# A PEER expert-choice stage: adaLN products spread between the key projections, and one-hot gate rows from a 16-bit comparison shared out anew

## The chip, the cores and the metric

The program runs on one core of one Trainium2 chip. Its engines work side by side and wait for each other by semaphores: TensorE (PE; its weight loads are PEld), VectorE (DVE), ScalarE (ACT), GpSimd (POOL), and SyncE (SP), which here only issues DMAs. The metric is the device time of one execution in microseconds (us). The numbers of before are the median of three timed executions, and one further execution taken by the profiler.

## The reference

One denoising step of a two-layer transformer over 640 tokens (512 latent, 128 context). Each layer has an attention mixer (differential attention in layer 0, latent attention in layer 1), then a PEER mixer: product-key retrieval of 16 experts out of 16384 for each of 8 heads. Each sub-layer is an RMS norm with a shift, a scale and a gate (adaLN) from a linear map of the conditioning vector. The part that matters here:

```python
def modulation(cvec, w, b):
    m = jax.nn.silu(cvec) @ w + b
    return [t[:, None, :] for t in jnp.split(m, 6, axis=-1)]

def peer(h, wq, sub_keys, u, v):
    ...
    def one(xb):
        q = (xb @ wq).reshape(TOK_BLOCK, PEER_HEADS, 2, PEER_HALF)
        s = jnp.einsum('thcd,hcnd->thcn', q, sub_keys, preferred_element_type=jnp.float32)
        top_s, top_i = lax.top_k(s, PEER_TOPK)
        ...
        fs, fi = lax.top_k(cand_s, PEER_TOPK)
        idx = jnp.take_along_axis(cand_i, fi, axis=-1)
        g = jax.nn.softmax(fs, axis=-1)
        ue = u[idx]
        a = jax.nn.gelu(jnp.einsum('td,thkd->thk', xb, ue, preferred_element_type=jnp.float32))
        ve = v[idx]
        return jnp.einsum('thk,thkd->td', (g * a).astype(xb.dtype), ve)
```

## The kernel before

Tokens lie in five blocks of 128 (`TB = 5`). Each layer runs a norm, its attention, a second norm, `expert_choice`, and `experts`. The last takes most of the time: for the first 384 tokens (`TD`) it computes all 16384 experts with matmuls and weights them by a gate table in DRAM, for the other 256 it gathers the chosen rows. `expert_choice` chooses the experts and builds that table. It has two stages, and every engine has its own hand-written instruction order in it.

**Selection.** TensorE runs 20 key projections, `project` (L1336), n = 0 to 19, four for each block of tokens. Each is 32 matmuls of 128x128 in f32. In the middle of projection n it also does `scores` (L1350) of projection n-1. ScalarE copies the queries (`query`, L1411) and the scores (`score`, L1419) out of PSUM; at n = 4, 9, 14 and 19 it also writes two look-up tables (`tables`, L1428), and at n = 8, 12, 16 and 20 an exponential (`exps`, L1439). VectorE runs `choose` for each block: top 16 of 128 scores in four chunks c (L1569 to L1585), then the candidates (L1595), the ranks (L1599), top 16 of the candidates, and `lookups` (L1549, L1550). GpSimd finishes the lookups of blocks 0 to 3 (L1500, L1503, L1505) from the tables; block 4's are done by VectorE. `finish` (L1529 to L1534) normalizes the gates of the block before, in the middle of `choose`.

**The adaLN halves.** Twelve pieces ("halves") of layer 1's adaLN map are computed in layer 0's `expert_choice` (`early`, h = 0 to 11), four in layer 1's. One half is `late_half`: 8 matmuls of 128x256 into 32 PSUM partitions each (`mod_rows`, L119), whose result ScalarE copies to `mrow` (`late_row`, L1435), and which two small matmuls then turn into columns (`late_turn`, `mod_turn`, L125). SyncE loads a half (1 MB, L1310) once the half two before it has been used. In the kernel before, all of them stand on TensorE behind the last projection and its scores; ScalarE copies four of them before the exponential of block 3, three before the tables of block 4, five after. VectorE adds the bias (L130) after its last block.

**Gate steps.** Then 32 steps (`STEPS`), each for 12 tokens (`SUB`), build the table. For every token a step needs two matrices of 128x128, which TensorE multiplies (L1388, 12 matmuls): `one1`, a comparison of first key numbers with 0 to 127 (tile `w`), and `one2`, the same for the second key numbers, times the gates (tile `pqT`). `one1` is VectorE's (L1651). Of the 12 tokens of `one2`, VectorE does 2 whole (L1649) and compares 6 more (L1645), which ScalarE scales by the gates (L1450), and GpSimd does 4 (L1512). ScalarE moves the product to a staging tile (`evict_g`, L1462), behind the scaling of the next step in its order; each pair of steps goes to DRAM as one DMA of 1.5 MB (L1318). There are two buffers of each operand and of the staging tile. With six steps to go (after pair 12 of 0 to 15) SyncE also starts two loads of 1 MB for the next stage (L1321).

The comparisons are in f32, and read the numbers 0 to 127 from PSUM (`iota_ps`) on VectorE and from SBUF (`iota`) on GpSimd.

Of the kernel before, what the change touches and what calls it, by code (L numbers as in the profile page):

```python
# [25 lines left out]
P = 128  # L26
# [34 lines left out]
def mixed(nc, cst, inp, outs, g_dram, x_dram):  # L61
# [1215 lines left out]
    def expert_choice(l, w3, pqT, keysT, selT, rows, gates, steps, sc, s2, cand, c2, vals, idxu, posu, idxp, ranks, posh,  # L1277
                      shift, fs, first, eq, tabs, sel, mrow):

# [14 lines left out]
        with nc.Block() as block:  # L1294
# [29 lines left out]
            def _(pe):  # L1324
# [40 lines left out]
                def late_turn(h):  # L1365

                    at = h - early[0]
                    pe.wait_ge(sem("late_row"), h + 1)
                    mod_turn(pe, ps[:, 7, 256 + 4 * at:260 + 4 * at], mrow[:, h % 2, :]).then_inc(sem("late_t"), 1)
# [37 lines left out]
            def _(act):  # L1407
# [22 lines left out]
                def late_row(h):  # L1430

                    act.wait_ge(sem("late_mm"), h + 1)
                    if h >= 2:
                        act.wait_ge(sem("late_t"), h - 1)
                    act.copy(mrow[:, h % 2, :], ps[:, 4 + 2 * (h % 2), 0:256]).then_inc(sem("late_row"), 1)  # L1435

# [40 lines left out]
                for h in early[4:7]:  # L1477
                    late_row(h)
                tables(TB - 1)
                for h in early[7:]:  # L1480
                    late_row(h)
                act.wait_ge(sem("late_t"), early[-1] + 1)
                act.copy(iota_ps, iota[:]).then_inc(sem("gm_iota"), 1)
# [11 lines left out]
            def _(pool):  # L1495
# [10 lines left out]
                for r in range(STEPS):  # L1506
                    t0 = r * SUB
                    pool.wait_ge(sem(n_ + "selT"), (t0 + SUB - 1) // P + 1)
                    if r >= 2:
                        pool.wait_ge(sem("gm_mm"), r - 1)  # L1510
                    for t in range(DIRECT + SCALED, SUB):
                        last = pool.tensor_scalar(one2[:, r % 2, t, :], iota[:], selT[:, 1, t0 + t:t0 + t + 1],  # L1512
                                                  selT[:, 2, t0 + t:t0 + t + 1], ALU.is_equal, ALU.mult)
                    last.then_inc(sem("gm_pool"), 1)

            @block.vector
            def _(v):
# [120 lines left out]
                def gate_step(r):  # L1638
                    t0 = r * SUB
                    v.wait_ge(sem("gm_iota"), 1)  # L1640
                    v.wait_ge(sem(n_ + "selT"), (t0 + SUB - 1) // P + 1)
                    if r >= 2:
                        v.wait_ge(sem("gm_mm"), r - 1)
                    n = SCALED
                    v.tensor_tensor(one2[:, r % 2, DIRECT:DIRECT + n],  # L1645
                                    selT[:, 1, t0 + DIRECT:t0 + DIRECT + n].unsqueeze(2).to_broadcast([P, n, P]),
                                    iota_ps.unsqueeze(1).to_broadcast([P, n, P]), ALU.is_equal).then_inc(sem("gm_eq"), 1)
                    for t in range(DIRECT):
                        v.tensor_scalar(one2[:, r % 2, t, :], iota_ps, selT[:, 1, t0 + t:t0 + t + 1],  # L1649
                                        selT[:, 2, t0 + t:t0 + t + 1], ALU.is_equal, ALU.mult)  # L1650
# [16 lines left out]
                v.wait_ge(sem("late_t"), early[-1] + 1)  # L1667
                add_bias(v, 1, k0, k0 + 2 * len(early), ps[:, 7, 256:256 + 4 * len(early)]).then_inc(sem("mod_v"), 1)
                if l == 0:
# [279 lines left out]
    def expert_layer(l):  # L1949
        with ExitStack() as st:  # L1950
# [3 lines left out]
            with ExitStack() as s2:  # L1954
# [7 lines left out]
                              sb(s2, f"first{l}", [P, 2, 16, 16], F16), sb(s2, f"eq{l}", [P, 2, HP, 16, 16], F16),  # L1962
                              sb(s2, f"tabs{l}", [P, 2, HP, 16, 16], F16), sb(s2, f"sel{l}", [P, TB, 2, HP, 16]), sb(s2, f"mrow{l}", [P, 2, 256]))

# [219 lines left out]
```

## Time and profile before

| what | us |
|---|---|
| median of three timed executions | 3924.34 |
| their range | 3922.66 to 3928.52 |
| the profiled execution | 3924.41 |
| its span, first to last instruction | 3922.6 |
| `expert_choice` of layer 0: projections start / first gate comparison / last gate matmul ends | 558.7 / 773.4 / 880.9 |

Rows come from the profiled execution, in us from the start of the span. The profile's page gives busy shares (PE 95%, DVE 83%, ACT 45%, POOL 28% of the span), which are means over stages with different limits. This stage is read in three kinds of view: windows, which give each engine's busy time and the granted clock of TensorE in a stretch; the timeline, which gives instructions in order with the idle time ahead of them and what ended it; and groups by line with the mean duration of one instruction. In the timeline a matmul in f32 shows as two records.

### The profile page before, as it was taken

What the parts mean: (1) busy time and instruction counts of PE and PEld (TensorE: products, weight loads), DVE (VectorE), ACT (ScalarE), POOL (GpSimd) and SP (SyncE); (2) the same over time, 40 slices, a digit from 0 to 9 for tenths busy, and PEclk for the clock granted to TensorE, in tenths of its full rate; (3) what the DMA queues carried; (4) which work ended last, traced back from release to release, by engine and by line L of the source; (5) the groups of instructions that cost most, each with busy time, mean ns of one, the idle gap of its engine ahead of it and who ended that gap; (6) DMA issues with size and microseconds to landing.
All of it is one profiled execution on the core that took longest, in us unless ns stands there. A gap on an engine that the chain in (4) does not pass through costs nothing. (4 is left out here: it accounts for less than half of the span.)

```text
span 3922.6 us, 55734 instructions
## 1 busy us (share of the span) xinstructions
PE 3731.2 (95%) x20637; PEld 3146.4 (80%) x20637; DVE 3239.0 (83%) x6793; ACT 1758.5 (45%) x2888; POOL 1117.1 (28%) x836
## 2 busy tenths in 40 slices
PE   8999999888999999999989999996899999999999
PEld 4546789688999999999854646896889999999998
DVE  5737639898999999999963636399899999999998
ACT  3315522394444444444423646223944444444443
POOL 0000003493333333333200000035833333333332
PEclk9999889799999999999989999897999999999999
DMA  7310030299999999999841010301999999999997
GB/s 300 140 43 12 22 128 2 108 251 409 421 413 408 405 406 404 404 405 406 326 175 52 1 43 22 128 2 51 266 426 418 413 409 404 404 406 403 406 405 296
DMA packets 268270, 1033.70 MB, mean 264 GB/s; under 512 B 147072, under 2 KB 150080, under 8 KB 159936
## 3 DMA queue, kind: packets, MB, share of 16 engines
q0 software_dynamic: 77184, 562.07, 35.7%
q1 hardware_dynamic: 190816, 468.07, 31.4%
q8 instruction: 165, 2.70, 0.3%
q14 instruction: 105, 0.86, 0.1%
HBM read 970.69 MB, written 59.39 MB: 263 GB/s over the span
## 5 line engine op out<-in xcount | busy, mean ns | idle before, releaser
L1727 POOL DMA_INDIRECT gbuf<-in_uv,rows x340 | 514.8, 1514 | 863.6 <-DVE hT L1911 793.8
L1911 DVE SCALAR_TENSOR_TENSOR hT<-gbuf,act,hT 128x1024 f32<-128x1024 f32 x336 | 416.9, 1282 | 6.0
L1896 DVE SCALAR_TENSOR_TENSOR gbuf<-gbuf,ht 128x1024 f32<-128x1024 f32 x340 | 402.0, 1219 | 11.5 <-DMA gbuf<-in_uv,rows 11.5
L1727 POOL DMA_INDIRECT xT<-in_uv,rows x172 | 256.9, 1494 | 473.0 <-DVE hT L1911 393.2
L1500 POOL TENSOR_TENSOR eq<-eq,tabs 128x4096 f16<-128x4096 f16 x8 | 63.5, 7940 | 1070.2 <-DVE eq L1550 981.3
L1743 PE MATMUL ps<-h0h,U0h 128*128 128x384 f32 x1024 | 345.0, 337 | 6.8 <-DVE U0l L1870 6.8
L1743 PE MATMUL ps<-h1h,U1h 128*128 128x384 f32 x1024 | 345.2, 337 | 6.0 <-DVE U1l L1870 6.0
L1743 PE MATMUL ps<-h1h,U1l 128*128 128x384 f32 x1024 | 344.5, 336 | 0.0
L1743 PE MATMUL ps<-h0h,U0l 128*128 128x384 f32 x1024 | 344.4, 336 | 0.0
L1743 PE MATMUL ps<-h1l,U1h 128*128 128x384 f32 x1024 | 344.3, 336 | 0.0
L1743 PE MATMUL ps<-h0l,U0h 128*128 128x384 f32 x1024 | 344.2, 336 | 0.0
L1816 ACT ACTIVATE ring<-ps 128x384 f32<-128x384 f32 x256 | 125.9, 492 | 392.4 <-PE ps L1743 392.3
L1826 ACT ACTIVATE act<-act 128x2 f32<-128x2 f32 x256 | 51.8, 202 | 444.7 <-DVE gbuf L1896 296.4
L1336 PE MATMUL ps<-hT,ring 128*128 128x128 f32 x1920 | 232.5, 281 | 6.1 <-ACT hT L317 4.5
L1336 PEld LDWEIGHTS ps<-hT,ring 128*128 128x128 f32 x1920 | 225.1, 196 | 10.8 <-ACT hT L317 5.7
L1388 PE MATMUL ps<-pqT,w 128*128 128x128 f32 x1536 | 190.6, 282 | 37.2 <-DVE w L1651 32.3
L1388 PEld LDWEIGHTS ps<-pqT,w 128*128 128x128 f32 x1536 | 180.5, 196 | 47.7 <-DVE w L1651 28.0
L1512 POOL TENSOR_SCALAR pqT<-iota,selT 128x128 f32<-128x128 f32 x256 | 203.8, 810 | 51.1 <-ACT selT L1443 28.4
L1896 DVE SCALAR_TENSOR_TENSOR xT<-xT,ht 128x1024 f32<-128x1024 f32 x172 | 203.5, 1220 | 9.6 <-DMA xT<-in_uv,rows 9.6
L1911 DVE SCALAR_TENSOR_TENSOR hT<-xT,act,hT 128x1024 f32<-128x1024 f32 x168 | 208.4, 1282 | 3.0
L1743 PEld LDWEIGHTS ps<-h0h,U0h 128*128 128x128 f32 x1024 | 193.5, 189 | 10.0 <-DVE U0l L1870 7.5
L1743 PEld LDWEIGHTS ps<-h1h,U1h 128*128 128x128 f32 x1024 | 193.9, 189 | 9.1 <-DVE U1l L1870 6.6
(392 smaller groups left out, 9150.3 us busy)
## 6 DMA issues: line engine op xcount, KB each, us to landing
ring<-in_u SPq DMA_DIRECT2D x128, 1024.0 KB, 12.5
ring<-in_v SPq DMA_DIRECT2D x128, 1024.0 KB
ring<-in_wts SPq DMA_DIRECT2D x26, 2048.0 KB, 8.8
gates<-ring SPq DMA_DIRECT2D x32, 1536.0 KB, 7.3
ring<-gates SPq DMA_DIRECT2D x64, 768.0 KB
abuf<-in_ada_mid POOLq DMA_DIRECT2D x16, 1024.0 KB, 5.1
xT<-in_ada_late SPq DMA_DIRECT2D x16, 1024.0 KB, 4.9
abuf_c<-in_ada_late POOLq DMA_DIRECT2D x8, 1024.0 KB, 5.1
```

The source lines that it names most:

```text
L1336: mm = pe.matmul(ps[:, 5 + n % 3, q * P:(q + 1) * P], w[:, dc, q * P:(q + 1) * P], hT[:, dc, tb * P:(tb + 1) * P], start=dc == 0, stop=dc ...
L1388: mm = pe.matmul(ps[:, b + t // 4, (t % 4) * P:(t % 4 + 1) * P], one1[:, r % 2, t, :], one2[:, r % 2, t, :], start=True, stop=True)
L1500: pool.tensor_tensor(eq4, eq4, tab4, ALU.mult).then_inc(look, 1)
L1512: last = pool.tensor_scalar(one2[:, r % 2, t, :], iota[:], selT[:, 1, t0 + t:t0 + t + 1], selT[:, 2, t0 + t:t0 + t + 1], ALU.is_equal, ALU ...
L1727: pool.indirect_dma_start(out=slots[m % GSLOTS], out_offset=None, in_=inp[f"uv{l}"], in_offset=bass.IndirectOffsetOnAxis(ap=rows[:, c:c + ...
L1743: mm = pe.matmul(up_bank(k), Us[x][:, k, dc * P:(dc + 1) * P], hs[y][:, dc, :], start=dc == 0 and x + y == 0, stop=dc == DC - 1 and x == 1)
L1816: act.activation(Wf[:, k, :], up_bank(k), ACT.Gelu_apprx_tanh).then_inc(sem(n_ + "gelu"), 1)
L1826: act.activation(act4[:, n % 2, 0:2], act4[:, n % 2, 0:2], ACT.Gelu_apprx_tanh)\
L1896: v.scalar_tensor_tensor(u, u, 1.0, ht[:, m // P, :], ALU.mult, ALU.mult, accum_out=act4[:, n % 2, m % 2:m % 2 + 1]).then_inc(sem(n_ + "do ...
L1911: v.scalar_tensor_tensor(y, x, w, y, ALU.mult, ALU.add).then_inc(sem(n_ + "acc"), 1)
```

## The change

Two edits in `expert_choice`.

The halves: `late_half(h)` now stands behind a projection, the first behind n = 6 (`FIRST_HALF`), one behind each after it: n = 6 to 17 in layer 0, n = 6 to 9 in layer 1. `late_half` begins with `late_turn` of the half before it. On ScalarE, `late_row` of a half stands behind `query` of the projection after it. All halves use PSUM bank 4.

The gate steps: VectorE compares 10 tokens at once in 16 bits (`hot`, in the space of `eq`), with the key numbers in `sel16` and the numbers 0 to 127 repeated ten times in `numbers`, both in SBUF. `hot` is laid out with the token innermost, so one token's 128 values lie 20 bytes apart. ScalarE scales tokens 0 to 3 from it, GpSimd tokens 4 to 9 in one multiplication with the gates broadcast, VectorE does tokens 10 and 11 whole as before. VectorE's new comparison waits for the readers of `hot` two steps back; its other work and ScalarE's scaling wait for the matmuls two steps back.

```diff
-        SUB, DIRECT, SCALED = 12, 2, 6
+        SUB, SCALED, HOT = 12, 4, 10
+        hot = eq[:].rearrange("p a h s k -> p (a h s k)")[:, 0:2 * P * HOT].rearrange("p (b n t) -> p b n t", b=2, n=P)
+        numbers = sc[:, 1].bitcast(F16).rearrange("p i k -> p (i k)")[:, 0:P * HOT].rearrange("p (n t) -> p n t", n=P)
+        FIRST_HALF = 6
...
                 def late_half(h):
 
-                    pe.wait_ge(sem(f"late_in{h % 2}"), 16 * (h // 2 + 1))
-                    if h - early[0] >= 2:
-                        pe.wait_ge(sem("late_row"), h - 1)
-                    mod_rows(pe, ps[:, 4 + 2 * (h % 2), 0:256], halves[:, h % 2]).then_inc(sem("late_mm"), 1)
                     if h != early[0]:
                         late_turn(h - 1)
+                    pe.wait_ge(sem(f"late_in{h % 2}"), 16 * (h // 2 + 1))
+                    mod_rows(pe, ps[:, 4, 0:256], halves[:, h % 2]).then_inc(sem("late_mm"), 1)
...
                     pe.wait_ge(sem("gm_one"), r + 1)
-                    pe.wait_ge(sem("gm_pool"), r + 1)
                     pe.wait_ge(sem("gm_scaled"), r + 1)
...
                     for t in range(SUB):
+                        if t == SCALED:
+                            pe.wait_ge(sem("gm_pool"), r + 1)
+                        if t == HOT:
+                            pe.wait_ge(sem("gm_direct"), r + 1)
...
                 for n in range(4 * TB):
                     project(n // 4, n % 4)
+                    if 0 <= n - FIRST_HALF < len(early):
+                        late_half(early[n - FIRST_HALF])
                 scores(TB - 1, 3)
-                for h in early:
-                    late_half(h)
...
                     act.wait_ge(sem(n_ + "t"), tb + 1)
+                    act.copy(sel16[:, tb * P:(tb + 1) * P], ps[:, 5, P:2 * P])
...
                     act.wait_ge(sem("gm_eq"), r + 1)
-                    for t in range(DIRECT, DIRECT + SCALED):
-                        at = act.activation(one2[:, r % 2, t, :], one2[:, r % 2, t, :], ACT.Identity,
+                    if r >= 2:
+                        act.wait_ge(sem("gm_mm"), r - 1)
+                    for t in range(SCALED):
+                        at = act.activation(one2[:, r % 2, t, :], hot[:, r % 2, :, t], ACT.Identity,
                                             scale=selT[:, 2, r * SUB + t:r * SUB + t + 1])
...
-                    if n == 4 * TB:
-                        for h in early[0:4]:
-                            late_row(h)
+                    if 0 <= n - FIRST_HALF - 1 < len(early):
+                        late_row(early[n - FIRST_HALF - 1])
...
-                    for t in range(DIRECT + SCALED, SUB):
-                        last = pool.tensor_scalar(one2[:, r % 2, t, :], iota[:], selT[:, 1, t0 + t:t0 + t + 1],
-                                                  selT[:, 2, t0 + t:t0 + t + 1], ALU.is_equal, ALU.mult)
-                    last.then_inc(sem("gm_pool"), 1)
+                    pool.tensor_tensor(one2[:, r % 2, SCALED:HOT], hot[:, r % 2, :, SCALED:HOT].rearrange("p n t -> p t n"),
+                                       selT[:, 2, t0:t0 + n].unsqueeze(2).to_broadcast([P, n, P]), ALU.mult)\
+                        .then_inc(sem("gm_pool"), 1)
...
                     if r >= 2:
+                        v.wait_ge(sem("gm_scaled"), r - 1)
+                        v.wait_ge(sem("gm_pool"), r - 1)
+                    v.tensor_tensor(hot[:, r % 2], sel16[:, t0:t0 + HOT].unsqueeze(1).to_broadcast([P, P, HOT]),
+                                    numbers, ALU.is_equal).then_inc(sem("gm_eq"), 1)
```

On TensorE, in layer 0's selection, before: the seventh and eighth projection (n = 6, 7), each with the scores of the one before in its middle, follow each other (L1336 is `project`, L1350 `scores`; names are output<-operands).

```order
L1336 MATMUL ps<-hT,ring 128x128 x16
L1336 MATMUL ps<-hT,w 128x128 x16
L1350 MATMUL ps<-keysT,pqT 128x128 x4
L1336 MATMUL ps<-hT,w 128x128 x16
L1336 MATMUL ps<-hT,ring 128x128 x16
L1350 MATMUL ps<-keysT,pqT 128x128 x4
```

Now, at the same place (`project` is L1339, `scores` L1353):

```order
L1339 MATMUL ps<-hT,ring 128x128 x16
L119 MATMUL ps<-xT,c_silu 32x256 x8
L1339 MATMUL ps<-hT,w 128x128 x16
L1353 MATMUL ps<-keysT,pqT 128x128 x4
L1339 MATMUL ps<-hT,w 128x128 x16
L125 MATMUL ps<-gains,mrow 128x2 x2
L119 MATMUL ps<-xT,c_silu 32x256 x8
L1339 MATMUL ps<-hT,ring 128x128 x16
```

Between two projections stand the columns of the last half (L125) and the rows of the next (L119).

On ScalarE, at the same place now (L1415 is `query`, L1423 `score`, L1439 `late_row`, L1443 `exps`):

```order
L1423 COPY sc<-ps 128x512
L1415 COPY pqT<-ps 128x512
L1439 COPY mrow<-ps 128x256
L1443 ACT_TABLE_LOAD
L1443 ACTIVATE fs<-fs 128x128
L1423 COPY sc<-ps 128x512
L1415 COPY pqT<-ps 128x512
L1439 COPY mrow<-ps 128x256
```

The copy of a half's rows stands behind the copy of the next projection's queries; before, these copies stood behind the last projection.

On VectorE, one gate step before, from the last adaLN instruction:

```order
L136 SCALAR_TENSOR_TENSOR mod<-mod,norms 128x16
L1645 TENSOR_TENSOR pqT<-selT,ps 128x768
L1649 TENSOR_SCALAR pqT<-ps,selT 128x128 x2
L1651 TENSOR_TENSOR w<-selT,ps 128x1536
L1645 TENSOR_TENSOR pqT<-selT,ps 128x768
```

And now (`eq` is the tile that holds `hot`, `sc` the one that holds `numbers`):

```order
L136 SCALAR_TENSOR_TENSOR mod<-mod,norms 128x16
L1646 TENSOR_TENSOR eq<-selT,sc 128x1280
L1650 TENSOR_TENSOR w<-selT,ps 128x1536
L1654 TENSOR_SCALAR pqT<-ps,selT 128x128 x2
L1646 TENSOR_TENSOR eq<-selT,sc 128x1280
```

The first comparison is larger and reads both operands from SBUF, and `one1` moved up to second place.

## Rows read from the trace of the kernel before

**Rows 1.** Windows: start:end, length, busy time (x records) per engine, granted clock, DMA.

```profile
558.70:727.40 168.70, 167.21 (x1444) 164.86 (x1448) 143.16 (x1012) 43.14 (x64) 47.83 (x15) 0.97 0.13 50
727.30:729.30 2.00, 1.98 (x34) 0.94 (x32) 1.96 (x17) 2.00 (x2) 0.00 (x0) 1.00 0.00 0
785.00:880.00 95.00, 86.59 (x714) 81.91 (x715) 92.92 (x117) 91.95 (x203) 90.58 (x117) 1.00 1.00 252
```

**Rows 2.** Timeline of TensorE behind layer 0's last projection: start, duration, instructions, [idle before <-releaser].

```profile
727.35 1.93 PE L119 MATMUL ps<-xT,c_silu 128*32 128x256 f32 x32
730.62 0.61 PE L125 MATMUL ps<-gains,mrow 128*128 128x2 f32 x4 [1.34 <-ACT mrow L1435]
733.36 1.93 PE L119 MATMUL ps<-xT,c_silu 128*32 128x256 f32 x16 [2.14 <-DMA xT<-in_ada_late]
```

**Rows 3.** Timeline of ScalarE, same place.

```profile
725.62 0.59 ACT L1411 COPY pqT<-ps 128x512 f32<-128x512 f32 x1 [2.99 <-PE ps L1336]
726.11 1.90 ACT L1428 CAST tabs<-ranks 128x2048 f16<-128x2048 f32 x1
...
735.36 0.37 ACT L1435 COPY mrow<-ps 128x256 f32<-128x256 f32 x1 [4.52 <-PE ps L119]
```

**Rows 4.** Timeline of VectorE, block 4 of layer 0 and the first gate comparison.

```profile
734.20 0.29 DVE L1571 MAX8 vals<-sc 128x8 f32<-128x128 f32 x1
...
739.73 2.44 DVE L1534 TENSOR_TENSOR gates<-fs,small 128x128 f32<-128x128 f32 x1
...
772.11 0.29 DVE L1529 TENSOR_REDUCE small<-fs 128x8 f32<-128x128 f32 x1 [8.66 <-ACT fs L1439]
...
773.41 0.95 DVE L1645 TENSOR_TENSOR pqT<-selT,ps 128x768 f32<-128x768 f32 x1
```

**Rows 5.** Timeline of GpSimd, the lookups of block 3.

```profile
729.95 7.94 POOL L1500 TENSOR_TENSOR eq<-eq,tabs 128x4096 f16<-128x4096 f16 x1 [23.94 <-ACT tabs L1428]
737.96 7.81 POOL L1503 TENSOR_TENSOR eq<-eq 128x2048 f16<-128x2048 f16 x3
```

**Rows 6.** Timelines of one gate step in mid-stage: VectorE, TensorE, ScalarE, GpSimd.

```profile
788.24 0.95 DVE L1645 TENSOR_TENSOR pqT<-selT,ps 128x768 f32<-128x768 f32 x1
789.11 0.72 DVE L1649 TENSOR_SCALAR pqT<-ps,selT 128x128 f32<-128x128 f32 x2
789.75 1.75 DVE L1651 TENSOR_TENSOR w<-selT,ps 128x1536 f32<-128x1536 f32 x1
791.41 0.95 DVE L1645 TENSOR_TENSOR pqT<-selT,ps 128x768 f32<-128x768 f32 x1
...
788.31 2.94 PE L1388 MATMUL ps<-pqT,w 128*128 128x128 f32 x24 [0.21 <-DVE w L1651]
...
788.14 1.44 ACT L1462 COPY ring<-ps 128x1536 f32<-128x1536 f32 x1
789.48 1.86 ACT L1450 ACTIVATE pqT<-pqT,selT 128x128 f32<-128x128 f32 x6
...
797.84 79.98 POOL L1512 TENSOR_SCALAR pqT<-iota,selT 128x128 f32<-128x128 f32 x100
```

**Rows 7.** Groups by line and shape, whole program: count, busy us, mean ns, idle before.

```profile
L1549 DVE TENSOR_TENSOR eq<-posh,first 128x2048 f16<-128x2048 f16 x10 | 12.3, 1226 | 0.3
...
L1503 POOL TENSOR_TENSOR eq<-eq 128x1024 f16<-128x1024 f16 x8 | 17.2, 2156 | 0.6
L1503 POOL TENSOR_TENSOR eq<-eq 128x512 f16<-128x512 f16 x8 | 9.6, 1202 | 0.6
...
L1803 ACT CAST U0h<-ring 128x1024 fp32r<-128x1024 f32 x128 | 133.6, 1044 | 5.0 <-DMA ring<-in_u 4.2 <-PEq L1294 0.8
...
L1835 ACT COPY hT<-ring 128x768 f32<-128x768 f32 x64 | 102.6, 1603 | 0.0
```

**Rows 8.** The table's DMAs (line L1318), and ScalarE's wait for one late in the stage.

```profile
DMA to landing us min/median/max: 7.0/7.3/13.0
...
883.65 2.78 ACT L1462 COPY ring<-ps 128x1536 f32<-128x1536 f32 x2 [5.90 <-DMA gates<-ring]
```

**Rows 9.** Timelines in layer 1: VectorE in block 4, TensorE's first two gate steps.

```profile
2696.17 1.93 DVE L1534 TENSOR_TENSOR gates<-fs,small 128x128 f32<-128x128 f32 x1
...
2724.34 8.17 PE L1388 MATMUL ps<-pqT,w 128*128 128x128 f32 x48 [14.84 <-DVE w L1651]
```

More of the change, by code:

```diff
@@ L1277, in expert_choice @@
     def expert_choice(l, w3, pqT, keysT, selT, rows, gates, steps, sc, s2, cand, c2, vals, idxu, posu, idxp, ranks, posh,
-                      shift, fs, first, eq, tabs, sel, mrow):
+                      shift, fs, first, eq, tabs, sel, mrow, sel16):
         n_ = "ch_"
@@ L1368, in late_turn @@
                     pe.wait_ge(sem("late_row"), h + 1)
-                    mod_turn(pe, ps[:, 7, 256 + 4 * at:260 + 4 * at], mrow[:, h % 2, :]).then_inc(sem("late_t"), 1)
+                    mod_turn(pe, ps[:, 4, 384 + 4 * at:388 + 4 * at], mrow[:, h % 2, :]).then_inc(sem("late_t"), 1)
                 def late_half(h):
-                    pe.wait_ge(sem(f"late_in{h % 2}"), 16 * (h // 2 + 1))
-                    if h - early[0] >= 2:
-                        pe.wait_ge(sem("late_row"), h - 1)
-                    mod_rows(pe, ps[:, 4 + 2 * (h % 2), 0:256], halves[:, h % 2]).then_inc(sem("late_mm"), 1)
                     if h != early[0]:
                         late_turn(h - 1)
+                    pe.wait_ge(sem(f"late_in{h % 2}"), 16 * (h // 2 + 1))
+                    mod_rows(pe, ps[:, 4, 0:256], halves[:, h % 2]).then_inc(sem("late_mm"), 1)
                 def gate_step(r):
@@ L1434, in late_row @@
                         act.wait_ge(sem("late_t"), h - 1)
-                    act.copy(mrow[:, h % 2, :], ps[:, 4 + 2 * (h % 2), 0:256]).then_inc(sem("late_row"), 1)
+                    act.copy(mrow[:, h % 2, :], ps[:, 4, 0:256]).then_inc(sem("late_row"), 1)
                 def exps(tb):
@@ L1476, in _ @@
                         tables(MATS.index(n))
-                for h in early[4:7]:
-                    late_row(h)
                 tables(TB - 1)
-                for h in early[7:]:
-                    late_row(h)
-                act.wait_ge(sem("late_t"), early[-1] + 1)
+                act.copy(numbers, iota[:].unsqueeze(2).to_broadcast([P, P, HOT]))
                 act.copy(iota_ps, iota[:]).then_inc(sem("gm_iota"), 1)
@@ L1506, in _ @@
                 for r in range(STEPS):
[L1507 to L1508 removed]
+                    t0, n = r * SUB + SCALED, HOT - SCALED
+                    pool.wait_ge(sem("gm_eq"), r + 1)
                     if r >= 2:
                         pool.wait_ge(sem("gm_mm"), r - 1)
[L1511 to L1514 removed]
+                    pool.tensor_tensor(one2[:, r % 2, SCALED:HOT], hot[:, r % 2, :, SCALED:HOT].rearrange("p n t -> p t n"),
+                                       selT[:, 2, t0:t0 + n].unsqueeze(2).to_broadcast([P, n, P]), ALU.mult)\
+                        .then_inc(sem("gm_pool"), 1)
             @block.vector
@@ L1642, in gate_step @@
                     if r >= 2:
-                        v.wait_ge(sem("gm_mm"), r - 1)
[L1644 to L1650, printed above, removed]
+                        v.wait_ge(sem("gm_scaled"), r - 1)
+                        v.wait_ge(sem("gm_pool"), r - 1)
+                    v.tensor_tensor(hot[:, r % 2], sel16[:, t0:t0 + HOT].unsqueeze(1).to_broadcast([P, P, HOT]),
+                                    numbers, ALU.is_equal).then_inc(sem("gm_eq"), 1)
+                    if r >= 2:
+                        v.wait_ge(sem("gm_mm"), r - 1)
                     v.tensor_tensor(one1[:, r % 2, 0:SUB], selT[:, 0, t0:t0 + SUB].unsqueeze(2).to_broadcast([P, SUB, P]),
@@ L1653, in gate_step @@
                      .then_inc(sem("gm_one"), 1)
+                    for t in range(HOT, SUB):
+                        last = v.tensor_scalar(one2[:, r % 2, t, :], iota_ps, selT[:, 1, t0 + t:t0 + t + 1],
+                                               selT[:, 2, t0 + t:t0 + t + 1], ALU.is_equal, ALU.mult)
+                    last.then_inc(sem("gm_direct"), 1)
                 normed(v, l, 1)
@@ L1667, in _ @@
                 v.wait_ge(sem("late_t"), early[-1] + 1)
-                add_bias(v, 1, k0, k0 + 2 * len(early), ps[:, 7, 256:256 + 4 * len(early)]).then_inc(sem("mod_v"), 1)
+                add_bias(v, 1, k0, k0 + 2 * len(early), ps[:, 4, 384:384 + 4 * len(early)]).then_inc(sem("mod_v"), 1)
                 if l == 0:
@@ L1962, in expert_layer @@
                               sb(s2, f"first{l}", [P, 2, 16, 16], F16), sb(s2, f"eq{l}", [P, 2, HP, 16, 16], F16),
-                              sb(s2, f"tabs{l}", [P, 2, HP, 16, 16], F16), sb(s2, f"sel{l}", [P, TB, 2, HP, 16]), sb(s2, f"mrow{l}", [P, 2, 256]))
+                              sb(s2, f"tabs{l}", [P, 2, HP, 16, 16], F16), sb(s2, f"sel{l}", [P, TB, 2, HP, 16]), sb(s2, f"mrow{l}", [P, 2, 256]),
+                              sb(s2, f"selT16{l}", [P, TD], F16))
             def pair(name, shape):
```

## The prediction, made before the changed kernel was run

> **What bounds the kernel now.** The change touches only `expert_choice`, so I read that stage in both layers, in three steps: windows for who is busy, the timeline for who ends each part last, groups by line for what single instructions cost.
>
> Selection, first window of [rows 1]: TensorE is busy 167.21 of 168.70 us at a granted clock of 0.97, so it has no gap to fill and whatever is put between projections makes the stretch longer. VectorE is busy 143.16 us there. It trails the scores a little: behind the last projection ScalarE writes two tables of 1.90 us, 1.8 apart [rows 3], and then the last scores (0.59 us, as the copy in the same rows), so these are ready at 726.11 + 3.6 + 0.6 = 730.3; VectorE starts on them at 734.20 [rows 4]. Its lead of work is thus 3.9 us. From there about 30 us of VectorE work remain.
>
> In those 30 us the twelve halves run on TensorE, at no cost to VectorE until the end: it then idles 8.66 us before 772.11, for an exponential that ScalarE does behind the last of the halves. The first gate comparison starts at 773.41 [rows 4]. Without that wait it would have started at 764.75. In layer 1 four halves are done long before VectorE is, and it has no such wait.
>
> Gate steps, third window of [rows 1] and [rows 6]: GpSimd does 100 of its instructions in 79.98 us without a gap, four per step, which is 3.20 us a step. VectorE needs 0.87 + 0.64 + 1.66 = 3.17 from start to start. A loop through ScalarE takes two steps: product 2.94, copy out (1.34 to the next start), six scalings 1.86, some 0.2 of handing over, 6.34 or 3.17 a step. Three engines are level at 3.2, and TensorE waits for VectorE's `one1`.
>
> **The halves.** One half costs TensorE 1.93 / 2 = 0.97 us at clock 1.00 [rows 1, 2]: two of them ran in 1.93. The single half at 733.36 took the same 1.93, after TensorE had stood idle 1.34 and 2.14 us. Between projections the clock is full, so I take 0.97, and 0.5 for the turn (0.61 with the overlap [rows 2]).
>
> Each turn now also waits. It stands right behind a projection, but the rows it turns are copied by ScalarE only behind the copy of that projection's queries: 0.49 to the next start, 0.37 for the rows [rows 3], 0.1 of handing over, about 0.96 us in which TensorE stands, with the half and the next projection queued behind. So the first half costs 0.97 and each further one 0.96 + 0.5 + 0.97 = 2.43.
>
> Layer 0: 0.97 + 11 x 2.43 = 27.7 us. Layer 1: 0.97 + 3 x 2.43 = 8.3 us. Everything that follows the last projection moves by that much, ScalarE's tables for block 3 and GpSimd's lookups of block 3 behind them [rows 5] among it. VectorE's instructions with two operands in SBUF are held while GpSimd works: `finish` took 2.44 us at 739.73 [rows 4] and ended when GpSimd's second lookup could have (4.06 of the 7.81 us behind 737.96), and 1.93 us in layer 1 [rows 9]. So VectorE gets past `finish`, candidates and ranks only with GpSimd's lookups, and these move by the whole 27.7 and 8.3. If VectorE were not held, it would still start the last scores no sooner than they come: 27.7 - 3.9 = 23.8, and 4.4.
>
> Layer 0's gates would then start at 764.75 + 27.7 = 792.4, which is 19.0 later than 773.41 (15.1 at least). In layer 1 the shift is 8.3 (4.4 at least). Together **+27.3 us** (19.5 to 27.3). The halves' loads (a longer wait, 2.14 us, stood ahead of one [rows 2]) are hidden now, which saves nothing beyond the 8.66 already counted.
>
> **The gate steps.** VectorE: 768 elements take 0.95 and 1536 take 1.75 [rows 6], so 1.04 ns each and 0.15 fixed. The f16 comparison of 2048 with two SBUF operands takes 1.226 [rows 7], 0.52 ns each and the same fixed part. 1280 make 0.82, or 0.74 start to start. VectorE then needs 0.74 + 1.66 + 0.64 = 3.04 a step.
>
> ScalarE: four scalings for six, but they read 20 bytes apart. The only strided read on this engine, L1835 with 16 bytes, takes 1603 ns for 768 elements; a dense cast of 1024 takes 1044 [rows 7], and 0.83 us would be the price of 768 dense ones. So 1.0 ns more each, 0.13 for 128. Four cost 1.24 dense and 1.74 strided; I take the latter. The loop is 2.94 + 1.34 + 1.74 + 0.15 = 6.17, or 3.09 a step. This is the bound.
>
> GpSimd: dense f16 products of 512 and 1024 elements take 1.20 and 2.16 us [rows 7], so 768 take 1.68. No row shows it read with a stride; with ScalarE's surcharge of 0.77 it would be 2.45. VectorE's next comparison now has both operands in SBUF and would be held by it, which makes the step 0.82 + 0.05 + GpSimd's time: 2.55 or 3.32. It binds above 2.2 us. I take GpSimd's own row, 1.68, and keep 3.32 for the range.
>
> Three engines get cheaper, and a step goes from 3.20 to 3.09. Not in all 32: the first two go at TensorE's low clock (8.17 us for two in layer 1 [rows 9]), and the last six are paced by DMA, since the loads for the next stage start there: ScalarE waits 5.90 us for a staging buffer, and a landing takes up to 13.0 instead of 7.3 [rows 8]. In mid-stage a buffer is free three steps less one copy after its DMA, 3 x 3.09 - 1.44 = 7.8 us, still above 7.3. So 24 steps x 0.11 x 2 layers = **-5.4 us** (+5.8 with GpSimd at 2.45).
>
> The first product of a layer: before, VectorE did 0.87 + 0.64 + 1.74 until `one1` was there, now 0.74 + 1.74. **-1.7 us** for two layers. The extra copies on ScalarE (`sel16`, `numbers`) lie in its idle time before the first gate comparison: it waits for VectorE there. If that cover were gone they would cost about 2 us a layer.
>
> **Sum.** 3924.4 (the profiled execution, 3924.41, and the median, 3924.34, agree) + 27.3 - 5.4 - 1.7 = **3944.6 us**.
>
> **Rivals.**
> (a) GpSimd's strided read holds VectorE: 3924.4 + 27.3 - 1.7 + 5.8 = 3955.8. For it: the stride surcharge on ScalarE. Against: GpSimd takes 1.9 ns an element where ScalarE takes 0.83, so a slower fetch may be hidden.
> The Trainium skill (GPSIMD Engine Reference, Performance pitfalls for Q7 kernels) says that a read whose byte step is above 8 costs about 2.9 cycles an element where it is 1.9 else. No trace here shows it. By that rule, an estimate: 0.64 us more, 2.32 in all, steps of 3.19, and the time 3949.5.
> (b) The turn does not wait: ScalarE's copy of the rows gets ahead in a way that I don't see. A further half then costs 1.47; 17.1 and 5.4 us, shifts of 8.5 and 5.4: 3924.4 + 13.9 - 7.1 = 3931.2, which is no measurable change. Against it speaks the order on both engines.
> (c) Faster: the halves vanish in VectorE's lead. If a place costs under 3.9 / 12 = 0.33 us, layer 0 gains its 8.66 us and layer 1 loses nothing: 3924.4 - 8.7 - 7.1 = 3908.6. It turns into a gain from about 1.1 us a place down. For it: TensorE's busy time is modelled and VectorE is the slower of the two per block. Against: the 0.97 of a half alone at full clock [rows 2].
> (d) The 16-bit comparison does not run at two elements a cycle (its runs are ten elements, those of L1549 sixteen): 1280 x 1.04 + 0.15 = 1.48, a step of 3.70, 24 us more than before in the gate steps: 3924.4 + 27.3 - 1.7 + 24 = 3974. Or GpSimd is above 3 us, with about the same result.
>
> **How the numbers follow.** Forecast 0.55; (a) 0.20; (b) 0.12; (c) 0.05; (d) 0.08. A change of under 0.2%, 7.8 us, can't be told from none. Slower: 0.55 + 0.20 + 0.08 = 0.83; same: 0.12; faster: 0.05. The range goes from (b) to beyond (a), 3930 to 3960, and leaves out (c) and (d), 0.13; the lower shifts of the halves (-7.8) lie in it.
>
> **What would show it.** TensorE waiting for `mrow` about 1 us behind each projection from n = 7 on; layer 0's first gate comparison at about 792 instead of 773.4, layer 1's 8 us later counted from its projections; GpSimd's product at 1.7 us and gaps between them; steps at 3.09 with TensorE released by ScalarE's scalings. The forecast fails if the turns don't wait, if VectorE's new comparison is above 1.0 us or is held, or if GpSimd's product is above 2.2 us.

## The result

The changed kernel takes 3948.89 us (median of four timed executions, 3945.52 to 3949.97); the kernel before took 3925.31 us (median of four) beside it. The ratio is 1.0055, with a 95% interval from 1.0039 to 1.0071: slower, by little but clear of the noise. The forecast was 3944.6 us, in a range of 3930 to 3960.

The profiled execution's span is 3947.0 us, 24.4 more than before. Each layer's `expert_choice` can be cut in two by the starts of three instructions: the first projection, the first gate comparison, and the first transposition of the next stage, `experts`. The rows of before that are not in the groups ahead are in the fence, from TensorE's timeline (first two rows layer 0, the others layer 1) and VectorE's.

```profile
558.73 3.46 PE L1336 MATMUL ps<-hT,ring 128*128 128x128 f32 x8 [2.26 <-ACT hT L317]
887.27 3.25 PE L1773 MATMUL ps<-consts,hT 128*128 128x128 f32 x16 [6.35 <-PEq L1294]
2514.76 11.44 PE L1336 MATMUL ps<-hT,ring 128*128 128x128 f32 x41 [2.26 <-ACT hT L317]
2720.74 0.94 DVE L1645 TENSOR_TENSOR pqT<-selT,ps 128x768 f32<-128x768 f32 x1
2834.39 3.65 PE L1773 MATMUL ps<-consts,hT 128*128 128x128 f32 x16 [5.11 <-PEq L1294]
```

The same six points of the changed kernel, layer 0 and then layer 1:

```profile
557.69 4.38 PE L1339 MATMUL ps<-hT,ring 128*128 128x128 f32 x10 [2.26 <-ACT hT L317]
793.66 0.82 DVE L1646 TENSOR_TENSOR eq<-selT,sc 128x1280 f16<-128x1280 f16 x1
905.24 3.31 PE L1776 MATMUL ps<-consts,hT 128*128 128x128 f32 x16 [6.03 <-PEq L1297]
2533.17 17.43 PE L1339 MATMUL ps<-hT,ring 128*128 128x128 f32 x96 [2.26 <-ACT hT L317]
2748.37 0.81 DVE L1646 TENSOR_TENSOR eq<-selT,sc 128x1280 f16<-128x1280 f16 x1
2857.88 3.65 PE L1776 MATMUL ps<-consts,hT 128*128 128x128 f32 x16 [5.70 <-PEq L1297]
```

| us | before | after | difference | forecast |
|---|---|---|---|---|
| layer 0, selection | 214.7 | 236.0 | +21.3 | +19.0 |
| layer 0, gate steps | 113.9 | 111.6 | -2.3 | -3.55 |
| layer 1, selection | 206.0 | 215.2 | +9.2 | +8.3 |
| layer 1, gate steps | 113.65 | 109.5 | -4.1 | -3.55 |

These make +24.1; the other 0.3 us lie outside the stage. Selection lost 30.5 us, the gate steps gave 6.4 back.

**Selection after.** TensorE's timeline in layer 0, in the middle of the inserted halves (L125 turns a half, L119 computes one):

```profile
651.15 0.61 PE L125 MATMUL ps<-gains,mrow 128*128 128x2 f32 x4 [0.95 <-ACT mrow L1439]
651.69 1.07 PE L119 MATMUL ps<-xT,c_silu 128*32 128x256 f32 x16
652.69 3.84 PE L1339 MATMUL ps<-hT,ring 128*128 128x128 f32 x32
656.37 1.06 PE L1353 MATMUL ps<-keysT,pqT 128*128 128x128 f32 x8
657.26 3.74 PE L1339 MATMUL ps<-hT,ring 128*128 128x128 f32 x32
661.95 0.61 PE L125 MATMUL ps<-gains,mrow 128*128 128x2 f32 x4 [0.95 <-ACT mrow L1439]
```

Behind every projection TensorE stands for 0.95 us until ScalarE has copied `mrow`. One projection with its half takes 661.95 - 651.15 = 10.80 us. Without one it took 657.53 - 649.49 = 8.04 us in the kernel before, from one second part to the next:

```profile
649.49 3.74 PE L1336 MATMUL ps<-hT,ring 128*128 128x128 f32 x32
653.06 3.74 PE L1336 MATMUL ps<-hT,w 128*128 128x128 f32 x32
...
657.53 3.74 PE L1336 MATMUL ps<-hT,w 128*128 128x128 f32 x32
```

A place, which is a turn and a half put between two projections, costs 2.76 us.

ScalarE's tables for block 3, and VectorE and GpSimd at the end of layer 0's selection, the counterpart of [rows 3] to [rows 5]:

```profile
755.90 1.90 ACT L1432 CAST tabs<-ranks 128x2048 f16<-128x2048 f32 x1
...
760.12 0.29 DVE L1572 MAX8 vals<-sc 128x8 f32<-128x128 f32 x1 [2.59 <-issue]
...
765.64 2.16 DVE L1535 TENSOR_TENSOR gates<-fs,small 128x128 f32<-128x128 f32 x1
767.93 6.65 DVE L1596 TENSOR_TENSOR cand<-vals 128x128 f32<-128x128 f32 x4
774.62 1.11 DVE L1600 TENSOR_TENSOR ranks<-idxp 128x128 f32<-128x128 f32 x1
...
759.74 7.91 POOL L1502 TENSOR_TENSOR eq<-eq,tabs 128x4096 f16<-128x4096 f16 x1 [34.70 <-ACT tabs L1432]
767.73 7.86 POOL L1505 TENSOR_TENSOR eq<-eq 128x2048 f16<-128x2048 f16 x3
```

`finish` ends at 767.80, 0.15 us behind the end of GpSimd's product (767.65); the ranks end at 775.73, 0.14 us behind the end of its third addition (775.59).

**Gate steps after.** ScalarE and TensorE in mid-stage, the counterpart of [rows 6]:

```profile
803.29 1.79 ACT L1457 ACTIVATE pqT<-eq,selT 128x128 f32<-128x128 f16 x4
804.99 1.42 ACT L1469 COPY ring<-ps 128x1536 f32<-128x1536 f32 x1
806.30 1.79 ACT L1457 ACTIVATE pqT<-eq,selT 128x128 f32<-128x128 f16 x4
808.13 1.44 ACT L1469 COPY ring<-ps 128x1536 f32<-128x1536 f32 x1
809.47 1.79 ACT L1457 ACTIVATE pqT<-eq,selT 128x128 f32<-128x128 f16 x4
...
811.35 5.94 PE L1392 MATMUL ps<-pqT,w 128*128 128x128 f32 x48 [0.25 <-issue]
```

ScalarE works without a gap: 809.47 - 803.29 = 6.18 us for two steps, 3.09 a step, and TensorE's next pair of steps follows at 817.55, 6.20 us later. By line and shape, over both layers (count, busy us, mean ns of one, idle before):

```profile
L1513 POOL TENSOR_TENSOR pqT<-eq,selT 128x768 f32<-128x768 f16 x64 | 121.2, 1893 | 115.6 <-DVE eq L1646 97.9 <-PE ps L1392 17.7
L1646 DVE TENSOR_TENSOR eq<-selT,sc 128x1280 f16<-128x1280 f16 x64 | 52.1, 814 | 0.0
L1457 ACT ACTIVATE pqT<-eq,selT 128x128 f32<-128x128 f16 x256 | 114.8, 523 | 21.5 <-DVE eq L1646 21.5
L1469 ACT COPY ring<-ps 128x1536 f32<-128x1536 f32 x64 | 91.4, 1432 | 18.2 <-DMA gates<-ring 12.9 <-PE ps L1392 4.3
```

### The profile page after: what moved, and what is told of

Its sections match the earlier page's. It is cut to its first block and busy times, and to the rows that moved or that the text cites. A ratio compares the mean times of both kernels' runs of the same rounds, so it can differ in the third digit from the quotient of the medians.

```text
span 3947.0 us, 55469 instructions
## 1 busy us (share of the span) xinstructions
PE 3717.4 (94%) x20637; PEld 3138.4 (80%) x20637; DVE 3236.4 (82%) x6793; ACT 1753.8 (44%) x2768; POOL 1033.9 (26%) x644
## 5 line engine op out<-in xcount | busy, mean ns | idle before, releaser
L1899 DVE SCALAR_TENSOR_TENSOR gbuf<-gbuf,ht 128x1024 f32<-128x1024 f32 x340 | 402.0, 1219 | 11.5 <-DMA gbuf<-in_uv,rows 11.5
L1339 PE MATMUL ps<-hT,ring 128*128 128x128 f32 x1920 | 234.3, 281 | 6.1 <-ACT hT L317 4.5
L1339 PEld LDWEIGHTS ps<-hT,ring 128*128 128x128 f32 x1920 | 224.9, 196 | 15.7 <-issue 10.0
L101 PE MATMUL ps<-hT,ring 128*128 128x512 f32 (+1 forms) x368 | 193.8, 609 | 5.0 <-ACT hT L317 5.0
## 6 DMA issues: line engine op xcount, KB each, us to landing
ring<-in_u SPq DMA_DIRECT2D x128, 1024.0 KB, 12.5
```

Source lines behind the costliest of these rows:

```text
L101: e.matmul(out[:, 0:512], lhsT, rhs[:, 0:512], start=start, stop=stop)
L1339: mm = pe.matmul(ps[:, 5 + n % 3, q * P:(q + 1) * P], w[:, dc, q * P:(q + 1) * P], hT[:, dc, tb * P:(tb + 1) * P], start=dc == 0, stop=dc ...
L1899: v.scalar_tensor_tensor(u, u, 1.0, ht[:, m // P, :], ALU.mult, ALU.mult, accum_out=act4[:, n % 2, m % 2:m % 2 + 1]).then_inc(sem(n_ + "do ...
```

## The experiments

Times are medians of timed executions, with the kernel before beside them on the same chip. Its median was 3923.38 us beside the first four kernels, 3924.13 beside the next four, and 3927.18 beside the last two. Stage lengths come from each kernel's profiled execution, between the same instructions as in the table above. A difference between kernels of different groups is good to a few us only, since the kernel before moved by up to 3.8 us between them.

### Each edit alone

`gates_only` is the change with all that concerns the halves put back:

```diff
                 for n in range(4 * TB):
                     project(n // 4, n % 4)
-                    if 0 <= n - FIRST_HALF < len(early):
-                        late_half(early[n - FIRST_HALF])
                 scores(TB - 1, 3)
+                for h in early:
+                    late_half(h)
```

> The new gate steps alone; the halves stand behind the last projection as before. My theory: the loss of the change is all the halves', and the gate steps gain what the trace of the change shows from the first gate comparison to the next stage, 2.3 us in layer 0 and 4.1 in layer 1. So 3925 - 6.4 = 3919 us, steps at 3.09 us. Rival: the gate steps lose too in some way (colder start, slower landings) and the time is 3925 or more. In layer 0 the first gate comparison stays at 773 to 774.

Measured: 3918.99 us, ratio 0.9984 (0.9975 to 0.9994). Selection takes 214.3 and 205.6 us, as before; the gate steps 109.8 and 111.2.

`halves_only` is the kernel before with the same lines moved the other way, ScalarE's copies with them, and the old gate steps.

> The new places of the halves alone, with the old gate steps at 3.20 us. My theory: selection gets longer by 21.3 us in layer 0 and 9.2 in layer 1, as in the trace of the change, so 3925 + 30.5 = 3955.5 us. Rival: the two edits interact (the space of eq, bank 4, the copies that ScalarE has more of), and the time is 3950 or less.

Measured: 3954.99 us, ratio 1.0085 (1.0063 to 1.0107). Selection takes 236.7 and 215.5 us, 22.0 and 9.5 more than before.

The two edits add up within the noise: -4.4 and +31.6 us against the kernel before beside them, 27.2 together, where the change measured +23.6. The gap of 3.6 us is smaller than the uncertainty of `halves_only` (8.6 us each way) or of the change (6.3 us). The stage lengths agree more closely: selection +31.5 us in `halves_only` and +30.5 in the change, gate steps -6.5 us in `gates_only` and -6.4 in the change. The gate steps are a gain, the halves are the whole loss.

### Without the turn's wait

```diff
                         if q == 1 and n:
                             scores((n - 1) // 4, (n - 1) % 4)
+                        if q == 1 and 0 <= n - 1 - FIRST_HALF < len(early):
+                            late_turn(early[n - 1 - FIRST_HALF])
...
-                    if h != early[0]:
-                        late_turn(h - 1)
...
                 for n in range(4 * TB + 1):
+                    if 0 <= n - FIRST_HALF - 1 < len(early):
+                        late_row(early[n - FIRST_HALF - 1])
                     if n:
                         score(n - 1)
                     if n < 4 * TB:
                         query(n)
-                    if 0 <= n - FIRST_HALF - 1 < len(early):
-                        late_row(early[n - FIRST_HALF - 1])
```

> The change, but each half is turned in the middle of the next projection, behind its scores, and ScalarE copies its rows ahead of those scores instead of behind the next queries. Nothing else moves. My theory: the turn's wait for ScalarE, 0.95 us at each of 11 and 3 places, goes, so TensorE's selection is 10.5 us shorter in layer 0 and 2.9 in layer 1, the whole 13.3 us shorter than the change: about 3935.5 us. Rival 1: the wait is replaced by one for the scores' bank or for the rows, and the time stays at 3948. Rival 2: VectorE is the bound in part and only 5 to 9 us are won.

Measured: 3934.17 us, ratio to before 1.0029 (1.0018 to 1.0039). That is 14.7 us under the change, or 12.8 if each is taken against the kernel before beside it; 13.3 was expected. Selection is 11.5 us shorter than the change's in layer 0 and 2.9 in layer 1. TensorE's timeline shows no wait, and projections 9.68 us apart:

```profile
643.65 0.51 PE L125 MATMUL ps<-gains,mrow 128*128 128x2 f32 x4
644.01 3.82 PE L1339 MATMUL ps<-hT,ring 128*128 128x128 f32 x32
647.76 1.07 PE L119 MATMUL ps<-xT,c_silu 128*32 128x256 f32 x16
648.76 3.84 PE L1339 MATMUL ps<-hT,ring 128*128 128x128 f32 x32
652.43 1.06 PE L1355 MATMUL ps<-keysT,pqT 128*128 128x128 f32 x8
653.33 0.51 PE L125 MATMUL ps<-gains,mrow 128*128 128x2 f32 x4
```

A place costs 9.68 - 8.04 = 1.64 us here: the turn 0.36, the half 1.00, and 0.28 by which the two parts of the projection are longer from start to start (3.75 and 3.67 us, 3.57 each before). So the wait and what goes with it is 1.12 of the 2.76, and the rest is work. Neither rival holds: nothing takes the wait's place, and VectorE keeps none of it back.

### GpSimd's hold on VectorE

```diff
-        MATS = (4, 9, 14, 19)
+        MATS = (4, 9, 14, 18)
```

> The change, but ScalarE writes the tables of block 3 behind n = 18 instead of 19, so that GpSimd's lookups of block 3 start about 9 to 11 us sooner and are done, or nearly so, when VectorE comes to finish, candidates and ranks. If VectorE is really held by GpSimd there (about 8.5 us above the undisturbed durations in layer 0, 7 in layer 1), these go, and the last scores come 2.9 us sooner since the tables no longer stand ahead of them: 10 us less in layer 0, 6 to 8 in layer 1, about 3932 us in all. Rival: these instructions are slow for another reason (VectorE at a later point of its own queue, the operands), and only the 2.9 us of the scores in layer 0 are won: 3945 us.

Measured: 3936.43 us, ratio to before 1.0035 (1.0025 to 1.0046). That is 12.5 us under the change, or 10.5 if each is taken against the kernel before beside it. Selection is 6.6 us shorter than the change's in layer 0 and 6.3 in layer 1. In layer 1 the change (three rows) and this kernel (four; GpSimd's last lookup is done at 2714.4):

```profile
2722.39 3.40 DVE L1535 TENSOR_TENSOR gates<-fs,small 128x128 f32<-128x128 f32 x1
2725.93 3.74 DVE L1596 TENSOR_TENSOR cand<-vals 128x128 f32<-128x128 f32 x4
2729.71 0.63 DVE L1600 TENSOR_TENSOR ranks<-idxp 128x128 f32<-128x128 f32 x1
```

```profile
2715.09 0.29 DVE L1535 TENSOR_TENSOR gates<-fs,small 128x128 f32<-128x128 f32 x1
2715.51 0.89 DVE L1596 TENSOR_TENSOR cand<-vals 128x128 f32<-128x128 f32 x4
2716.45 0.29 DVE L1600 TENSOR_TENSOR ranks<-idxp 128x128 f32<-128x128 f32 x1
...
2713.77 0.66 POOL L1507 TENSOR_TENSOR sel<-eq 128x256 f32<-128x256 f16 x1
```

7.77 us of VectorE become 1.47 once GpSimd is idle, and the selection is shorter by just that 6.3. The hold is real and was on the path, and the rival, under which layer 1 would have gained nothing, is excluded. I had put 10 us on layer 0, and 6.6 came: there GpSimd still works while VectorE passes, so the same instructions take 5.16 us instead of 9.92 and 3.7 us of the hold remain. That gives 4.8 us; the other 1.8 I put down to the sooner last scores.

### What sets a gate step

Both kernels are `gates_only` with one number changed, the tokens that ScalarE scales (`SCALED`); GpSimd takes the others of ten.

```diff
-        SUB, SCALED, HOT = 12, 4, 10
+        SUB, SCALED, HOT = 12, 2, 10
```

> The kernel with the new gate steps alone, but ScalarE scales 2 tokens and GpSimd 8 (was 4 and 6). If VectorE's comparison is held while GpSimd multiplies, a step is 0.82 + 0.05 + GpSimd's time, which grows from 1.89 to about 2.37: 3.24 us, some 7 us more than 3919, and VectorE's comparison shows durations above 0.82. If nothing is held, VectorE's own 3.04 sets the step, and it is 3.04 to 3.09: 3916 to 3919.

Measured: 3924.3 us, ratio 0.9998 (0.9987 to 1.0008). GpSimd's product takes 2.46 us, VectorE's comparison 0.99 instead of 0.81, and the step 3.22:

```profile
826.43 0.99 DVE L1654 TENSOR_TENSOR eq<-selT,sc 128x1280 f16<-128x1280 f16 x1
...
829.65 0.98 DVE L1654 TENSOR_TENSOR eq<-selT,sc 128x1280 f16<-128x1280 f16 x1
...
824.28 2.46 POOL L1521 TENSOR_TENSOR pqT<-eq,selT 128x1024 f32<-128x1024 f16 x1 [0.76 <-DVE eq L1654]
```

The comparison starts at 826.43, GpSimd ends at 826.74 (824.28 + 2.46), and the comparison ends 0.68 us after that. It is held, as rival (a) had it. With a GpSimd product of 1.90 us (`gates_only`) it is not, nor with one of 2.19 (the last kernel below, whose comparison takes 0.818 us on average).

> The kernel with the new gate steps alone, but ScalarE scales 5 tokens and GpSimd 5. If ScalarE's engine time is what sets the step (its copy and scalings back to back, 0.43 from start to start of one scaling of values 20 bytes apart), the step is 1.34 + 5 x 0.43 = 3.49 us and the time some 17 us more than 3919. If VectorE or TensorE sets it, it stays under 3.2.

Measured: 3932.24 us, ratio 1.0020 (1.0010 to 1.0030), 13 us above `gates_only`. I had expected 3.49 and 17. ScalarE is without a gap, and a step takes 831.09 - 827.67 = 3.42 us:

```profile
827.67 1.53 ACT L1471 COPY ring<-ps 128x1536 f32<-128x1536 f32 x1
828.99 2.31 ACT L1459 ACTIVATE pqT<-eq,selT 128x128 f32<-128x128 f16 x5
831.09 1.53 ACT L1471 COPY ring<-ps 128x1536 f32<-128x1536 f32 x1
```

VectorE's `one1` waits 0.29 us for a product in each step there. So ScalarE sets the step from four scalings up, GpSimd at eight tokens and not yet at seven, and the split 4 / 6 / 2 stands near the corner of both.

### The price of the stride

```diff
-                        at = act.activation(one2[:, r % 2, t, :], hot[:, r % 2, :, t], ACT.Identity,
+                        at = act.activation(one2[:, r % 2, t, :], flat[:, r % 2, t * P:(t + 1) * P], ACT.Identity,
...
-                    pool.tensor_tensor(one2[:, r % 2, SCALED:HOT], hot[:, r % 2, :, SCALED:HOT].rearrange("p n t -> p t n"),
+                    pool.tensor_tensor(one2[:, r % 2, SCALED:HOT], flat[:, r % 2, SCALED * P:HOT * P].rearrange("p (t n) -> p t n", t=n),
```

> The kernel with the new gate steps alone, but ScalarE and GpSimd read values of the comparison that lie next to each other, not 20 bytes apart. These are not the values of their tokens, so this kernel leaves the transposition of the comparison out and its gate table is not the reference's. It prices the stride. My theory: ScalarE's scaling goes from 0.523 back to 0.391 us as in the kernel before, GpSimd's product from 1.89 to 1.68, and the step from 3.09 to VectorE's own 3.04, so 2 to 3 us less than 3919. Rival: the 16-bit source is what makes them slower, not the stride, and nothing changes.

Measured: 3911.8 us, ratio 0.9961 (0.9946 to 0.9976).

Two groups of this kernel, GpSimd's and ScalarE's (count, busy us, mean ns of one, idle before):

```profile
L1522 POOL TENSOR_TENSOR pqT<-eq,selT 128x768 f32<-128x768 f16 x64 | 94.1, 1471 | 148.4 <-DVE eq L1655 142.1 <-PE ps L1395 6.2
L1460 ACT ACTIVATE pqT<-eq,selT 128x128 f32<-128x128 f16 x256 | 81.7, 393 | 13.8 <-DVE eq L1655 13.8
```

ScalarE's scaling costs 0.130 us more with the stride (0.523 against 0.393), GpSimd's product 0.42 (1.893 against 1.471). It is the stride, not the 16-bit source. VectorE's comparisons come 3.04 us apart.

The gate stages take 107.8 and 107.6 us, 5.7 less than those of `gates_only` together, where 2 to 3 were expected. A cost that I had missed explains most of it. In mid-stage of `gates_only` ScalarE waits 0.2 to 0.5 us for a staging buffer three times in layer 0 and four times in layer 1, and as it has no time to spare, each wait lengthens the stage: the steps take 3.14 us on average there in layer 0, not 3.09. With dense reads ScalarE has time to spare. It waits 26.1 us for staging buffers in all instead of 12.8, but the steps in mid-stage average 3.03 us, and only the last wait of each stage comes on top (6.33 and 6.04 us instead of 4.80 and 5.19).

### Fewer halves between projections

If a place costs 1.5 to 1.6 us without the wait, and a half behind the last projection some 3.4 us (TensorE waits there for the loads of the halves, as at 733.36 in [rows 2]), some places between projections should pay in layer 0 and none in layer 1. Both kernels have the new gate steps, the tables of block 3 behind n = 18, and the turn in the middle of the next projection; in layer 1 all halves stand behind the last projection as before.

```diff
-        MATS = (4, 9, 14, 19)
+        MATS = (4, 9, 14, 18)
...
-        FIRST_HALF = 6
+        FIRST_HALF, BETWEEN = 12, (6, 0)[l]
...
-                    if 0 <= n - FIRST_HALF < len(early):
+                    if 0 <= n - FIRST_HALF < BETWEEN:
                         late_half(early[n - FIRST_HALF])
                 scores(TB - 1, 3)
+                for h in early[BETWEEN:]:
+                    late_half(h)
```

> The new gate steps; block 3's tables behind n = 18; in layer 0 six of the twelve halves stand between projections (behind n = 12 to 17, turned in the middle of the next one), six behind the last, in layer 1 all four behind the last as in the kernel before. My theory: layer 1 gains GpSimd's hold (6.3 us, as measured with the tables moved), and in layer 0 six places of 1.5 us cost 9 us of TensorE, of which VectorE's lead takes some 6, while the tail of the halves ends 6 x (3.37 - 1.47) = 11 us sooner: the first gate comparison comes about 204 us behind the first projection instead of 214.3. So 3919 - 10 - 6.3 = 3903 us. Rival: VectorE has so little lead in the blocks before that each place still moves it: layer 0 stays at 210 or more, 3909 us.

Measured: 3905.1 us, ratio 0.9947 (0.9931 to 0.9964). Selection takes 207.1 and 199.9 us; 204 was expected in layer 0. VectorE has no wait before the gates there, so it is the bound at that point.

With four, behind n = 14 to 17:

> As the one with six between, but four in layer 0 (behind n = 14 to 17), eight behind the last projection. My theory: the tail of the halves decides and ends 4 x 1.9 = 7.6 us sooner than in the kernel before: layer 0's selection at 207, 3905 us, 2 us above the one with six. Rival: VectorE decides in both, and four are better than six by up to 3 us.

Measured: 3900.95 us, ratio 0.9940 (0.9924 to 0.9957). Selection takes 206.1 and 200.1 us. With four, VectorE waits 1.44 us in layer 0 for ScalarE, behind the last of the halves, so the tail decides, as expected; with six it doesn't wait. The two ends have nearly met. Six move VectorE and win nothing for it. The intervals overlap, and of the 4.2 us between the medians the selection explains 1.0; the profiled gate stages, in which the two kernels are the same, differ by 2.8. So the order of the two isn't shown by the times.

The third adds the split 3 / 7 / 2 in the gate steps:

> As the one with four halves between projections, but five (behind n = 13 to 17), and 3 tokens for ScalarE and 7 for GpSimd in the gate steps. Selection of layer 0 about as with four, 205 to 207 us. The step: ScalarE 1.34 + 3 x 0.43 = 2.63, GpSimd 0.82 + 0.05 + 2.17 = 3.04, VectorE 3.04: 3.05 us, 24 x 0.04 x 2 = 2 us less, 3899 us. Rival: with VectorE and GpSimd level each holds the other at times, and the step stays at 3.09 or above: 3901 or more.

Measured: 3900.07 us, ratio 0.9934 (0.9917 to 0.9950). Selection takes 205.8 and 199.9 us, and VectorE's comparisons come 3.04 us apart. The step is as computed. The gate stages take 109.0 and 109.2 us, against 109.2 and 110.2 with four halves between, so 1.2 us less of the 2 expected: the waits for staging buffers in mid-stage now fall where ScalarE has time to spare, but its last wait of each stage grows from 5.27 and 4.96 to 5.81 and 6.37 us. In time the kernel can't be told from the one with four. Both beat the kernel before by 0.6 to 0.7%, and the change by 1.2%.

No kernel was run with the new gate steps, the earlier tables and all halves behind the last projection. So how much of these gains in layer 0 is due to the halves' place and how much to the tables is not shown.

## Why the prediction was right

**The halves' place: right, mis-sized.** I had 0.96 + 0.5 + 0.97 = 2.43 us for a place; it measured 2.76. The wait (0.95) and the turn (0.54 from start to start) are as said. The half takes 1.00, and 0.27 us more lie in the projection around it: its first part takes 3.68 us to the next start where one without a half in front takes 3.57, and the last 0.17 of its second part no longer overlaps with what follows. The stop for `mrow` is not needed for this: in the kernel with the turn in the middle TensorE doesn't stop, and the projection still loses 0.28 us. I had counted the inserted instructions only. Over 11 and 3 places that term is 3.6 and 1.0 us, and the miss in the table was 2.3 and 0.9.

**What follows moves with it: right.** The tables moved by 755.90 - 726.11, or 30.8 us counted from the first projection, and the first gate comparison by 21.3, which is 30.8 less the 8.66 of the old wait and 0.9. Most of this would have come without GpSimd: VectorE starts the last scores at 760.12 instead of 734.20, which is 27.0 us later counted from the first projection, or 30.8 less the 3.9 us that it had to spare. The hold brought back 3.1 of these 3.9, since `finish`, candidates and ranks take 9.9 us where they took 6.8. The kernel with earlier tables shows the hold as a cause and not as a mere coincidence.

**VectorE and ScalarE in a gate step: right.** The comparison takes 0.814 us (0.82 said), one scaling 0.13 more with the stride (0.13 said, from the gate copy L1835 of `experts` [rows 7]), the step 3.09 (3.09 said). Four scalings and the copy alone fill ScalarE (1.70 to 1.83 and 1.31 to 1.34 us from start to start); I had described it as a loop through the product. That both come to 3.09 is luck. `g_act5` tells them apart: the loop would give (2.94 + 1.32 + 2.10 + 0.15) / 2 = 3.26 us a step, ScalarE's own work 1.32 + 2.10 = 3.42, and 3.42 was measured.

**GpSimd's product: wrong in both parts, right in the verdict.** 1.89 us for 1.68. Dense it would be 1.47, less than the rows of in-place f16 sums gave, and the stride costs 0.42, not the 0.77 of ScalarE's row. By the rule of the Trainium skill (GPSIMD Engine Reference, Performance pitfalls for Q7 kernels), about one cycle an element, an estimate gives 0.64; the measurement decides for 0.42. Two errors of opposite sign met here (0.21 too much for the dense product, nothing for the stride), which is luck too. The product stayed under 2.2 us, and so VectorE was not held.

**The gate steps' sum: right over both layers** (6.4 us, 7.1 said), with an odd split. The sum has two small slips: 24 x 0.11 x 2 is 5.3 and not 5.4, and 3.25 - 2.48 us for the first `one1`, twice, is 1.5 and not 1.7. The first product starts 2.79 us behind the first comparison instead of 3.60, so that term measured 0.8 us a layer, though it is ScalarE's scalings that release it now. I had not counted waits of ScalarE for staging buffers in mid-stage, three of 0.5 us in layer 0 and four of 0.2 in layer 1, where my margin was 0.5 us over the median landing (which rose from 7.3 to 7.7). The split comes from the first two steps, which took 8.36 us of TensorE in layer 0, against 7.26 in layer 1:

```profile
796.45 8.36 PE L1392 MATMUL ps<-pqT,w 128*128 128x128 f32 x48 [12.37 <-ACT pqT L1457]
...
2751.17 7.26 PE L1392 MATMUL ps<-pqT,w 128*128 128x128 f32 x48 [12.48 <-ACT pqT L1457]
```

In the kernel before they took 7.37 and 8.17 us. Without the first product and the time ahead of it, the gate stages gained 2.5 and 2.4 us, so the layers are alike. The difference is TensorE's clock: over the 7 us from the start of the product its granted clock averages 0.59 in layer 0 (796.45 to 803.45) and 0.75 in layer 1 (2751.17 to 2758.17). In `gates_only` the layers stand the other way round (clock 0.75 and 0.58, product 7.23 and 8.41 us, stage 109.8 and 111.2). The idle time ahead doesn't decide it: it was 12.37 and 12.48 us in the changed kernel. What decides when the clock rises stays open.

**The rivals.** (b) is excluded by TensorE's 0.95 us waits. (c), the halves hidden in VectorE's lead, needed a place under 0.33 us, and one costs 2.76. (d) is excluded by the comparison's 0.814 us. (a) was the closest: its mechanism exists, and `g_pool8` shows it at 2.46 us.

## What to carry to other kernels

Work put between the instructions of an engine that has no gaps costs its full time, and a consumer placed right behind a producer on another engine costs the round trip each time: compute between two instructions of the full engine, but consume half a stage later. Before spreading a tail out, ask what the tail costs where it stands; here the halves cost 8.7 us of waiting at the end of layer 0's selection and 21.3 us more than that when spread. With the earlier tables, four to six of the twelve between projections gave selections of 205.8 to 207.1 us; smaller numbers were not tried. When three engines are level, price each of them for the new split from rows with the same stride and type, because a gain goes only down to the next of them, and then to the DMA queue. An engine with no time to spare also passes on every short wait that another would absorb.

## What the runs showed of the hardware

Reading f16 values 20 bytes apart instead of side by side cost ScalarE 0.130 us per 128 elements (1.0 ns each) and GpSimd 0.42 us per 768 (0.55 ns each).

VectorE's instructions with two SBUF operands were held until GpSimd's instruction in progress was done: four small additions took 6.65 us beside GpSimd and 0.89 without. A reduction and a reciprocal with one operand, at 765.11 and 765.40 beside GpSimd's product, took no longer than elsewhere (0.26 and 0.20 us, against 0.29 and 0.20 at 772.11 and 772.43 in the kernel before).

A turn and a half between projections make the projection around them 0.27 us longer beyond their own 0.54 and 1.00 us (0.28 us beyond 0.36 and 1.00 where the turn stands in the middle).

After nearly the same idle time (12.37 and 12.48 us), two equal products of 48 matmul records took 8.36 and 7.26 us, with a granted clock of 0.59 and 0.75 over their first 7 us.
